# The first pair of FFN columns moved from plain matmuls into the seven products of the down projection

## What is computed

```
x = x + 0.5 * ((silu(rms(x) @ w1_gate) * (rms(x) @ w1_up)) @ w1_down)
x = x + mix(rms(x))        # attention and mLSTM heads, then @ w_out
x = x + 0.5 * ((silu(rms(x) @ w2_gate) * (rms(x) @ w2_up)) @ w2_down)
y = rms(x) * g_final
```

## Time and profile before

| | us |
|---|---|
| median of 3 runs | 2008.4 (2005.64 to 2012.96) |
| the profiled execution's own time | 2008.43 |
| its span, first to last instruction | 2006.5 |
| TensorE busy | 1957.0 |
| VectorE, GpSimd, ScalarE busy | 1305.8, 1031.0, 768.8 |

### The profile page before, as it was taken

How to read it: one execution, slowest core, us unless ns; L and a number is a source line. 1 busy time by engine, 2 the same in 40 slices (tenths; PEclk the granted TensorE clock), 3 DMA queues, 4 the chain that set the end, 5 groups by cost and what they waited for, 6 DMA issues and landing times.

```text
span 2006.5 us, 39074 instructions
## 1 busy us (share of the span) xinstructions
PE 1957.0 (98%) x14597; PEld 1911.0 (95%) x14597; DVE 1305.8 (65%) x1906; ACT 768.8 (38%) x1567; POOL 1031.0 (51%) x938
## 2 busy tenths in 40 slices
PE   7999999999999999999999999999999999999998
PEld 7999999999999998989998999999999999999997
DVE  6766777766667677764445664867777667656674
ACT  6423333333243344743333642343333333233333
POOL 2277777774466561132212443247777777455661
PEclk8999999999999999999999999999999999999999
DMA  8133545435764630333322745215354344666542
GB/s 263 65 129 130 179 134 179 146 128 170 256 183 142 195 97 4 94 109 106 95 82 72 195 121 121 76 55 181 133 179 149 128 160 150 199 205 196 171 144 100
DMA packets 218877, 281.97 MB, mean 141 GB/s; under 512 B 16072, under 2 KB 154344, under 8 KB 218768
## 3 DMA queue, kind: packets, MB, share of 16 engines
q1 hardware_dynamic: 211072, 260.87, 41.1%
q0 software_dynamic: 7696, 19.63, 3.1%
HBM read 190.50 MB, written 89.89 MB: 140 GB/s over the span
## 4 chain that ended last, share of the span: by engine, by line
PE 88%; DVE 3%; POOL 3%; DMA 2%; ACT 2%; issue 2%; SPq 0%; DVEq 0%; ACTq 0%; POOLq 0%
PE bank L279 27%; PE bank L281 27%; PE bank L280 27%; PE bank L2511 1%; PE bank L2530 1%; POOL X L1438 1%; PE bank L2521 1%; DMA WRAW<-in_w_down 1%; DMA XIN<-in_x_prompt 1%; DMA WS<-in_w_down 0%; PE bank L2452 0%; PE bank L2619 0%; PE bank L1301 0%; PE bank L1299 0%; PE bank L1300 0%
## 5 line engine op out<-in xcount | busy, mean ns | idle before, releaser
L279 PE MATMUL bank<-HA,HW 128*128 128x272 f32 x1008 | 291.9, 290 | 8.7 <-POOL HA L1362 8.7
L281 PE MATMUL bank<-HA,HW 128*128 128x272 f32 x1008 | 291.8, 289 | 0.0
L280 PE MATMUL bank<-HA,HW 128*128 128x272 f32 x1008 | 290.6, 288 | 0.0
L1356 DVE SCALAR_TENSOR_TENSOR HW<-WRAW,HW 128x512 fp32r<-128x512 f32 x126 | 208.0, 1690 | 121.3 <-ACT HW L1351 121.0
L1362 POOL TENSOR_TENSOR HA<-ARAW,HA 128x544 fp32r<-128x544 f32 x126 | 200.8, 1616 | 148.2 <-ACT HA L1350 148.2
L279 PE MATMUL bank<-HH,WGH 128*128 128x362 f32 (+2 forms) x808 | 264.0, 327 | 2.9 <-DVE HL L341 2.9
L280 PE MATMUL bank<-HL,WGH 128*128 128x362 f32 (+2 forms) x808 | 255.3, 316 | 0.0
L281 PE MATMUL bank<-HH,WGL 128*128 128x362 f32 (+2 forms) x808 | 254.8, 315 | 0.0
L279 PE MATMUL bank<-FC,WR 128*128 128x272 f32 x768 | 224.2, 292 | 3.2 <-ACT X L795 2.7
L281 PE MATMUL bank<-FC,WR 128*128 128x272 f32 x768 | 223.0, 290 | 0.0
L280 PE MATMUL bank<-FC,WR 128*128 128x272 f32 x768 | 222.3, 289 | 0.0
(11 more groups left out here) (376 smaller groups left out, 5840.7 us busy)
## 6 DMA issues: line engine op xcount, KB each, us to landing
asp<-SA SPq DMA_DIRECT2D x44, 544.0 KB, 3.4
RAWG<-in_w_gate SPq DMA_DIRECT2D x22, 1024.0 KB, 6.5
RAWU<-in_w_up SPq DMA_DIRECT2D x22, 1024.0 KB, 6.3
tsp<-TT SPq DMA_DIRECT2D x36, 544.0 KB, 5.4
ARAW<-tsp SPq DMA_DIRECT2D x72, 272.0 KB, 3.3
WS<-in_w_down SPq DMA_DIRECT2D x18, 1024.0 KB, 8.6
wsp<-WS SPq DMA_DIRECT2D x18, 1024.0 KB, 8.5
WRAW<-wsp SPq DMA_DIRECT2D x72, 256.0 KB, 3.9
```

The lines of the kernel that those rows point to most:

```text
L279: nc.tensor.matmul(bank[:, 0:w], w_hi, rhs_hi, start=first, stop=False)
L280: nc.tensor.matmul(bank[:, 0:w], w_hi, rhs_lo, start=False, stop=False)
L281: return nc.tensor.matmul(bank[:, 0:w], w_lo, rhs_hi, start=False, stop=last)
L1356: nc.vector.scalar_tensor_tensor(out=HW[f][h][:, 1], in0=WRAW[r][:, :], scalar=0.5, in1=HW[f][h][:, 0].bitcast(F32), op0=ALU.mult, op1=ALU ...
```

## The change

Pair 0 joins the scheme: `MID` becomes 10, there are 70 tiles, and groups are always two tiles. Its differences are made from the reloaded activations AR0 in stage (10, up, 0); its weight sums, and those of pair 1, which before stood in the second stage of all, move to stages (10, gate, 1) and (10, up, 0), in tiles of their own, WS0 and WS1. The plain matmuls of pair 0 and their evictions go. Tiles 0 and 1 are split inside stage (10, up, 1); tiles 2 on wait for the last up matmul. Each of GpSimd's four calls of `pool_quadrants` becomes two single instructions with two tiles between them.

```diff
-MID = PAIRS - 2
-SETS = ((0, 2), (2, 2), (4, 2), (6, 3))
+MID = PAIRS - 1
+SETS = tuple((k, 2) for k in range(0, MID, 2))
...
         def load_sums(sp, f, p, w):
-            n = MID * f + p - 1
+            ws = w[p * 2 * P:(p + 1) * 2 * P, :].rearrange("(k p) (d c) -> p k d c", p=P, d=2)
             if p == 1:
-                sp.wait_ge(st.tlo, 8 * f + 8)
-            sp.wait_ge(down_ws_io, WS_FROM + 32 * n)
...
+                sp.dma_start(WS1[:, :, :, :], ws).then_inc(s_.d_in, 16)
+                return
+            sp.wait_ge(down_ws_io, WS_FROM + WS_PER * f + 32 * sums_turn(p))
+            sp.dma_start((WS if p else WS0)[:, :, :, :], ws).then_inc(down_ws_io, 16)
...
         def tile_pair(t):
-            return t // MID, t % MID + 1
+            return t // MID, (t % MID + 1) % MID
...
             sp.wait_ge(s_.lo, 140 * f + 14 * LAST - 7)
-            load_d(sp, 0, w_down)
+            load_sums(sp, f, 0, w_down)
             for j in range(2):
                 store_differences(sp, f, LAST - 1, j)
...
             load_a(sp, f, 0, AR0)
+            sp.wait_ge(s_.lo, 140 * f + 14 * LAST)
+            load_sums(sp, f, 1, w_down)
+            store_sums(sp, f, 0)
+            for j in range(2):
+                store_differences(sp, f, 0, j)
+            for j in range(2):
+                sp.wait_ge(s_.a_out1 if j else s_.a_out0, 176 * f + 160)
+            sp.wait_ge(down_ws_io, WS_FROM + WS_PER * f + 32 * (MID - 1))
+            for t in range(RAWS):
+                load_tile(sp, f, t, w_down)
             sp.wait_ge(s_.mm, 280 * f + 28 * LAST - 14 + 4)
             reload(sp, f, 0)
+            store_sums(sp, f, 1)
             store_a(sp, f, LAST, 0)
             sp.wait_ge(s_.mm, 280 * f + 28 * LAST - 7 + 4)
+            load_tile(sp, f, RAWS, w_down)
             reload(sp, f, 1)
+            load_tile(sp, f, RAWS + 1, w_down)
             sp.wait_ge(s_.mm, 280 * f + 280)
             reload(sp, f, 2)
             store_a(sp, f, LAST, 1)
...
             load_d(sp, LAST, w_down)
...
+            dve_stage(dve, f, LAST, 1, 0, last=True, before=0)
+            dve_stage(dve, f, LAST, 1, 1, last=True, ahead_of=lambda: tile_weight_low(dve, f, 0), extra=lambda: tile_weight_low(dve, f, 1))
...
-            pool_stage(pool, f, 1, 0, 1, first=True, extra=lambda: down_sums(pool, f, 1))
...
+            pool_stage(pool, f, LAST, 0, 1, last=True, extra=lambda: down_sums(pool, f, 0))
+            pool_stage(pool, f, LAST, 1, 0, last=True, extra=lambda: down_sums(pool, f, 1))
+            pool_stage(pool, f, LAST, 1, 1, last=True, extra=first_tiles)
...
-            elif h < 4:
+            elif t < 2:
+                act.wait_ge(s_.mm, 280 * f + 28 * LAST - 7 + 1)
+            else:
                 act.wait_ge(s_.mm, 280 * f + 280)
...
+        QUADRANT_AFTER = {MID + 2: (0, 0), MID + 4: (0, 1), 4 * MID + 2: (1, 0), 4 * MID + 4: (1, 1),
+                          4 * MID + 6: (2, 0), 4 * MID + 8: (2, 1), 6 * MID + 2: (3, 0), 6 * MID + 4: (3, 1)}
...
         def down_pe(pe, f):
-            for n in range(3):
-                pe_down(pe, f, 0, n)
             for q in range(7):
                 pe_product(pe, f, q)
```

More of the change, by code:

```diff
@@ L409, in tile_group @@
         def tile_group(t):
-            q, p = tile_pair(t)
-            return 4 * q + [g for g, (i0, n) in enumerate(SETS) if i0 <= p - 1 < i0 + n][0]
+            return len(SETS) * (t // MID) + t % MID // 2
         def load_tile(sp, f, t, w):
@@ L724, in down_sums @@
         def down_sums(pool, f, p):
-            n = p * 4 + (4 * MID * f - 4)
-            b00, b10, b01, b11 = WS[:, 0, 0], WS[:, 0, 1], WS[:, 1, 0], WS[:, 1, 1]
-            pool.wait_ge(down_ws_io, p * 32 + (WS_FROM + 32 * MID * f - 16))
+            turn = sums_turn(p)
+            n = turn * 4 + 4 * MID * f
+            ws = WS if not isinstance(p, int) or p > 1 else (WS0, WS1)[p]
+            b00, b10, b01, b11 = ws[:, 0, 0], ws[:, 0, 1], ws[:, 1, 0], ws[:, 1, 1]
+            if isinstance(p, int) and p == 1:
+                pool.wait_ge(s_.d_in, 32 * f + 16)
+            else:
+                pool.wait_ge(down_ws_io, turn * 32 + (WS_FROM + WS_PER * f + 16))
             nc.gpsimd.tensor_tensor(b11, b10, b11, ALU.add).then_inc(down_ws, 1)
@@ L1203, in up_dve @@
                     dve_stage(dve, f, p, i // 2, i % 2, before=None if i else p - 1)
-            for i in range(3):
-                dve_stage(dve, f, LAST, i // 2, i % 2, last=True, before=None if i else LAST - 1)
-            def first_a():
-                for i in range(2):
-                    down_a_low(dve, nc.vector.tensor_tensor, f, 0, i)
-            def first_weight():
-                for i in range(2):
-                    down_low(dve, f, 0, i)
-            dve_stage(dve, f, LAST, 1, 1, last=True, ahead_of=first_a, extra=first_weight)
+            dve_stage(dve, f, LAST, 0, 0, last=True, before=LAST - 1)
+            dve_stage(dve, f, LAST, 0, 1, last=True)
+            dve_stage(dve, f, LAST, 1, 0, last=True, before=0)
+            dve_stage(dve, f, LAST, 1, 1, last=True, ahead_of=lambda: tile_weight_low(dve, f, 0), extra=lambda: tile_weight_low(dve, f, 1))
         def up_pool(pool, f):
@@ L1217, in up_pool @@
             weight_sum_last(pool, f, 1, 0, True)
-            pool_stage(pool, f, 1, 0, 0, first=True)
-            pool_stage(pool, f, 1, 0, 1, first=True, extra=lambda: down_sums(pool, f, 1))
+            for j in range(2):
+                pool_stage(pool, f, 1, 0, j, first=True)
             for j in range(2):
@@ L1261, in down_low, with last_high @@
-        def down_low(dve, f, e, i):
-            dve.wait_ge(s_.dhi, 2 * plain(f, e) + i + 1)
-            if not e:
-                dve.wait_ge(s_.mm, 280 * f + 28 * LAST - 7 + 2 + i + 1)
-            if by_token(f, e):
-                nc.vector.scalar_tensor_tensor(out=WB[e][:, 1, i], in0=RAWD[:, i], scalar=0.5, in1=WB[e][:, 0, i].bitcast(F32),
+        def last_high(act, f, i, what):
+            act.wait_ge(down_px, 8 * f + 6)
+            if what == "a":
+                act.wait_ge(s_.a_in, 32 * f + 32)
+                nc.scalar.activation(AB[:, 0, i], AR1[f][:, i], ACT.Copy).then_inc(s_.ahi, 1)
+            else:
+                act.wait_ge(s_.d_in, 32 * f + 32)
+                nc.scalar.activation(WB[:, 0, i], RAWD[:, i], ACT.Copy, scale=0.5 if f else 1.0).then_inc(s_.dhi, 1)
@@ L1327, in pe_down, with dve_x @@
                     between()
-        def dve_x(dve, f, e, n, tiles=range(KT)):
+        def dve_x(dve, n, tiles=range(KT)):
             t0, w = NTILE[n]
-            if not e:
-                dve.wait_ge(x_in[n], 16 * f + 32)
             for m in tiles:
                 i = 8 * n + m
-                x = (X2, X)[f][:, m, t0:t0 + w]
-                dve.wait_ge(s_.dmm, 24 * plain(f, e) + i + 1)
+                x = X2[:, m, t0:t0 + w]
+                dve.wait_ge(s_.dmm, i + 1)
                 nc.vector.scalar_tensor_tensor(out=x, in0=BANK[DOWN_BANK[i % 6]][:, 0:w], scalar=0.5, in1=x,
@@ L1440, in down_act @@
         def down_act(act, f):
-            act.wait_ge(s_.mm, 280 * f + 280)
-            for t in range(TILES):
+            for t in range(2, TILES):
                 tile_high(act, f, t)
-                if t == MID + 2:
+                if t == MID + 1:
                     act_product(act, f)
-            act.wait_ge(s_.a_out0, 176 * f + 176)
-            act.wait_ge(s_.a_out1, 176 * f + 176)
             for what in ("a", "w"):
                 for i in range(2):
-                    down_high(act, f, 1, i, what)
+                    last_high(act, f, i, what)
@@ L1462, in down_pool @@
             for i in range(2):
-                down_a_low(pool, nc.gpsimd.tensor_tensor, f, 1, i)
+                last_a_low(pool, f, i)
         def down_dve(dve, f):
-            for n in range(3):
-                dve_x(dve, f, 0, n)
-                if n < 2:
-                    for t in (2 * n, 2 * n + 1):
-                        tile_weight_low(dve, f, t)
-            for t in range(4, TILES):
+            for t in range(2, TILES):
                 tile_weight_low(dve, f, t)
-                if t % MID == 2 and t > 2 * MID - 1:
+                if t % MID == 1 and t > 2 * MID:
@@ L1865, in _ @@
             act.wait_ge(st.dg, NB + 2)
[L1866 removed]
+            act.wait_ge(s_.dmm, 24)
             def normed_root(i):
```

233 lines of the change are left out of this document (107 added, 126 removed).

## The result

The changed kernel takes 2016.99 us (median of 7 runs, 2013.25 to 2020.59) against 2008.47 for the kernel before (7 runs): a ratio of 1.0036, 95% interval 1.0022 to 1.0051. The forecast was a fall of 1.3 us; the median rose by 8.5. (The ratio, with its interval, is not the quotient of the medians: by it the rise is 7.2 us, between 4.4 and 10.2.) That lies inside the stated range and within 0.5%, but the interval leaves no doubt of the sign, and the forecast had the other one. The profiled execution took 2013.83 us.

The account below looks back on a forecast made before the run. TensorE was taken as the bound, busy 1957.0 of 2006.5 us. Hand-over cost 19.8, less 11.7 for quadrant-sum waits and 9.4 for early weight sums, gave -1.3: 2007.1 us from 2008.4, range 1992 to 2020.

Parts of the forecast that it names:

- 9.9 a half: Hand-over from up stages to tiles: later tiles start 8.4 us later, plus 1.5 us at half clock; 19.8 in all.
- the early sums: Pair 1's weight sums leaving the second stage: a 4.6 us wait and 4.8 us of low clock go, 9.4 us.
- WS1's issue: Last up stages: SyncE may load pair 1's weights at 494.0, possibly an us earlier.
- The wait for bank 5: Last up stage: bank 5 is free at 507.9, TensorE wants it at 504.14, so it waits 3.8 us.
- The wait for tiles 6 and 7: Hand-over: TensorE finishes six tiles, then waits some 6 us because these loads queue behind large copies on SyncE.
- Tile 7's landing: SyncE's queue: 15.2 MB at 383 GB/s takes 39.7 us, plus 2.3 latency, so the load lands at 536.0.
- The rest has cover: Beyond the hand-over: seven more tiles a half cost GpSimd 1.49 us and VectorE 1.6 each, beside TensorE's 3.02; no loss.
- I take the wait as gone: 11.7: Spreading GpSimd's quadrant sums removes 8.7 us of waits for tile splits and 3.0 us of half-clock loss.
- With it the low clock, 4.8: After TensorE's waits for VectorE's weight splits: half of 6.4 and 3.3 us low-clock stretches is regained, 4.8 us.
- The first: Rival at the hand-over: tiles do not queue behind large copies, small loads get through; 1992.9 us, chance 0.22.
- The second: Rival: TensorE's clock stays low through the hand-over, +11 us a half, 2029 us; chance 0.09.
- The third: Rival: quadrant sums still hold the tiles, so the 11.7 us stay; 2018.8 us, chance 0.09.

Follow-up runs that it names:

- the separate runs: Kernel before with only the quadrant sums spread: 1995.53 us, ratio 0.9937; kernel before with only pair 1's weight sums cut to 8 columns: 2003.79 us, ratio 0.9964.

## Why the prediction was wrong

**What failed is the size of the term "9.9 a half"**, the hand-over: it measured 13.1 us in f = 0 and 12.1 in f = 1, 25.2 in all in place of 19.8. These 5.4 us are most of the 7.1 between the forecast's -1.3 and the 5.8 by which the two profiled spans differ; 2.0 more are the early sums, 7.4 in place of 9.4. The mechanism was right: the tiles wait behind the large copies in SyncE's queue, as moving the copies out and back in shows (12.2 us less, 11.7 more). Step by step in f = 0, with the 5.0 us (504.14 to 499.15) by which it is earlier after:

*WS1's issue* was forecast at 494.0 - 5.0 = 489.0 and came at 487.76, the earlier bound. *The wait for bank 5* was forecast as 3.8 and is 1.74: the load landed at 493.76, the four sums took 5.2 us. *Tiles 1 to 3*: 2.4 forecast, 0.80 + 0.84 + 0.65 = 2.3 measured. *Half clock behind tile 7*: 3.2 us at 0.54, 1.5 lost, as forecast; that is luck, since in f = 1 none follows tile 7. SyncE and GpSimd:

```profile
487.76 0.37 SPq L401 DMA_DIRECT2D WS<-in_w_down  x1
...
508.54 4.19 SPq L433 DMA_DIRECT2D ARAW<-asp  x1
...
522.18 0.96 SPq L434 DMA_DIRECT2D WRAW<-in_w_down  x1
```

```profile
493.76 1.29 POOL L759 TENSOR_TENSOR WS<-WS 128x512 f32<-128x512 f32 x1 [10.76 <-DMA WS<-in_w_down]
```

*The wait for tiles 6 and 7*, some 6 us, came as 3.58 for tile 5, 1.79 for tile 6 and 1.15 for tile 7, 6.5 together.

*Tile 7's landing* is the first step that failed. It was forecast 2.3 + 39.7 = 42.0 us after WS1's issue. ScalarE begins to split the tile at 532.72, 45.0 after 487.76. Tile 4, the other row, was issued at 506.33 behind the first residual piece and two stores, and split at 516.27.

```profile
516.27 0.66 ACT L1350 ACTIVATE HA<-ARAW 128x544 fp32r<-128x544 f32 x1 [8.12 <-DMA WRAW<-in_w_down]
...
532.72 0.66 ACT L1350 ACTIVATE HA<-ARAW 128x544 fp32r<-128x544 f32 x1 [0.24 <-DMA WRAW<-in_w_down]
```

Two stretches show where the 3.0 us went:

```profile
487.76:490.00 2.24, 2.24 (x20) 2.24 (x19) 2.21 (x7) 0.41 (x2) 0.00 (x0) 1.00 0.53 49
490.00:532.72 42.72, 34.67 (x242) 33.38 (x241) 11.89 (x19) 8.82 (x17) 24.28 (x23) 0.92 1.04 376
```

The first 2.24 us move next to nothing, as the forecast's 2.3 of latency had it. At 376 GB/s in place of 383, the sum's 15.2 MB would have been through 0.4 us later than forecast (0.1 MB of them had moved by 490). The rest is bytes: 49 x 2.24 and 376 x 42.72 make 16.2 MB. The other 1.0 MB, 2.6 us, must be of transfers issued after tile 7 (tiles 8 and 9 and pair 10's activations, all issued by 528.2): they moved beside it, and the sum counted the bytes ahead of it alone. So tile 7 started 1.9 us later than 538.9 - 5.0 = 533.9, at 535.82.

*"The rest has cover"* is the second step that failed: tiles 12 and 13 were named nowhere. ScalarE stands in the product's copies until 549.5 and splits both only then; on GpSimd the first quadrant sum stands between the two. TensorE waits 0.80 us for tile 13 and 0.21 us at 562.79, and a stop costs a little more than its idle time (the one of 1.74 us stands between starts 499.02 and 501.05, 2.03 apart where the pace is 0.13). With 1.9 us for tile 7 that makes about 3.2.

```profile
549.15 0.40 ACT L1429 ACTIVATE U<-bank 128x272 f32<-128x272 f32 x1 [0.35 <-PE bank L283]
```

```profile
551.50 3.00 POOL L1441 TENSOR_TENSOR X<-X,U 128x1088 f32<-128x1088 f32 x1
```

**The two gains.** "I take the wait as gone: 11.7" held: 12.7 alone. "With it the low clock, 4.8" was the part least safe: the run with the early sums cut small gives 7.0 in place of 9.4 (4.8 to 9.8), and one profile shows these very waits at full clock. The 4.8 was also too much for the stretches that it was read from: matmuls at half clock start 0.227 us apart (525.34 to 528.06 are twelve) against 0.126, so they lose 44% of a stretch and not half, and the stretch of 6.4 us holds the second wait, of 0.57, which the 4.6 counts already. That "the first weights that were late are early by more than 3" was right in the change, which has no wait there.

**The sum redone** from the two profiles: 25.2 - 11.6 (the quadrant sums' 5.8 a half) - 7.4 = +6.2 us. With 0.9 us less ahead of 41.40 and 0.6 more between the halves, which are not the change's, that is the spans' 5.8 within rounding. With the prices of the separate runs it is 25.2 - 12.7 - 7.0 = +5.5, against 7.2 (4.4 to 10.2) by the ratio and 8.5 by the medians.

**The rivals.** The first, that small loads get through between large copies, did not come: they waited some 10 us. Its time of 1992.9 was reached only where the copies were taken out of the way. The second asked for a clock that stays low for over 12 us; it fell for about 3 us three times in f = 0, and the first two lie ahead of tile 7, whose landing sets the time whatever TensorE does before. In f = 1 it fell twice:

```profile
1750.70:1754.10 3.40, 3.05 (x13) 3.08 (x14) 1.98 (x5) 1.18 (x2) 3.32 (x5) 0.50 1.03 371
1767.80:1774.50 6.70, 5.63 (x25) 5.66 (x26) 0.93 (x1) 0.00 (x0) 0.38 (x1) 0.50 1.05 401
```

The third, quadrant sums that hold the tiles, is not in the change beyond the 0.80 and 0.21 us above, but is in the run that puts them together.

**On the page's figure.** The Trainium skill, "DMA: Bandwidth & Descriptors", section Specifications, gives a core about 358 GB/s of HBM, a stack's bandwidth divided by its two cores. This program runs on one core; the stretch of 40 us shows 374, and single stretches 387 and 408, so by the trace the engines moved more, and the forecast's rate was too high by 2% only.
